# One instruction instead of four for the high part of a split weight chunk, in a one-layer hybrid trunk

## What is computed

```python
def hybrid_layer(h, p, t5_table):
    xn = rms_norm(h, p["g_pre_mix"])
    z = xn @ p["w_in"] + p["b_in"]
    ...
    y_a = gla_branch(gla_q, gla_k, gla_v, gla_r, gla_a, p) @ p["w_br_gla"]
    y_b = dsa_branch(dsa_cq, dsa_ckv, idx_k, idx_w, p, t5_table) @ p["w_br_dsa"]
    y_c = mlstm_branch(ml_q, ml_k, ml_v, ml_o, ml_i, ml_f, p) @ p["w_br_ml"]
    mix = jax.nn.sigmoid(gate_a) * y_a + jax.nn.sigmoid(gate_b) * y_b + jax.nn.sigmoid(gate_c) * y_c
    h = h + rms_norm(mix @ p["w_out"], p["g_post_mix"])
    xn = rms_norm(h, p["g_pre_mlp"])
    u = jnp.square(jax.nn.relu(xn @ p["w_up"]))
    return h + rms_norm(u @ p["w_down"], p["g_post_mlp"])
```

## Time and profile before

| what | value |
|---|---|
| median of 3 runs | 1406.42 us (1404.33 to 1410.87) |
| the profiled execution, its own time | 1403.23 us |
| its span, from first to last instruction | 1401.5 us |
| mean granted TensorE clock | 0.984 |
| TensorE matmuls busy | 1354.8 us, 97% |
| VectorE busy | 592.5 us, 42% |
| GpSimd busy | 894.7 us, 64% |

### The profile page before, as it was taken

One profiled execution on the slowest core, in us unless ns is written; L12 is line 12 of the kernel. 1 busy time (PEld: TensorE's weight loads), 2 busy tenths in 40 slices (PEclk: granted clock), 3 DMA queues, 4 the chain that ended last, 5 costly groups with the idle time before them and its releaser, 6 DMA issues.

```text
span 1401.5 us, 18053 instructions
## 1 busy us (share of the span) xinstructions
PE 1354.8 (97%) x6611; PEld 1065.3 (76%) x6611; DVE 592.5 (42%) x1135; ACT 387.9 (28%) x796; POOL 894.7 (64%) x1452
## 2 busy tenths in 40 slices
PE   6999899999999999999999999999989999999997
PEld 4866666657887877778887787788768888888886
DVE  3147888541364756622463654223151111222224
ACT  4333365430012333233131331241241111121322
POOL 8475500005764553658884775689678888999992
PEclk9998899999999999999999999999999999999999
DMA  6862200002321211222331321243223333222221
GB/s 174 213 229 61 61 1 1 16 0 70 97 71 38 74 46 46 75 62 76 105 100 52 97 76 54 75 154 117 90 64 102 90 101 109 90 101 95 90 91 60
DMA packets 165710, 116.54 MB, mean 83 GB/s; under 512 B 11832, under 2 KB 146078, under 8 KB 165622
## 3 DMA queue, kind: packets, MB, share of 16 engines
q1 hardware_dynamic: 161142, 108.43, 26.5%
q10 hardware_dynamic: 4480, 6.95, 1.6%
HBM read 113.21 MB, written 7.52 MB: 86 GB/s over the span
## 4 chain that ended last, share of the span: by engine, by line
PE 83%; DVE 9%; DMA 3%; POOL 2%; issue 1%; ACT 1%; SPq 0%; DVEq 0%; ACTq 0%; POOLq 0%
PE GP L1588 38%; PE PA L1624 8%; PE GP L1624 6%; PE GP L1603 6%; PE GP L1585 5%; PE GP L1764 3%; PE PA L1809 3%; PE PA L1732 3%; DMA wraw<-in_w_in 3%; POOL wlo L559 1%; PE GP L1762 1%; PE GP L1749 1%; PE PA L1807 1%; DVE S L1120 1%; PE PA L1796 1%
## 5 line engine op out<-in xcount | busy, mean ns | idle before, releaser
L554 POOL TENSOR_SCALAR whi<-wraw 128x256 fp32r<-128x256 f32 x712 | 345.3, 511 | 380.2 <-PE GP L1588 208.7
L559 POOL TENSOR_TENSOR wlo<-wraw,whi 128x256 fp32r<-128x256 f32 x712 | 540.6, 791 | 14.8
L1588 PE MATMUL GP<-xh,whi 128*128 128x512 f32 x368 | 153.0, 416 | 2.9 <-DVE xl L1080 1.4
L1588 PE MATMUL GP<-xl,whi 128*128 128x512 f32 x368 | 148.1, 402 | 0.0
L1588 PE MATMUL GP<-xh,wlo 128*128 128x512 f32 x368 | 147.3, 400 | 0.0
L1588 PE MATMUL GP<-nh,whi 128*128 128x512 f32 x256 | 101.2, 395 | 0.7 <-DVE nl L1525 0.7
L1588 PE MATMUL GP<-nl,whi 128*128 128x512 f32 x256 | 101.3, 396 | 0.0
L1541 DVE TENSOR_TENSOR ul<-U,uh 128x512 fp32r<-128x512 f32 x64 | 48.3, 792 | 123.1 <-ACT uh L1010 123.1
L1588 PE MATMUL GP<-nh,wlo 128*128 128x512 f32 x256 | 99.8, 390 | 0.0
L1545 DVE TENSOR_TENSOR U<-U 128x512 f32<-128x512 f32 x32 | 26.0, 811 | 149.9 <-ACT U L1014 149.9
L1588 PEld LDWEIGHTS GP<-xh,whi 128*128 128x128 f32 x368 | 71.1, 193 | 21.4 <-issue 3.0
(11 more groups left out here) (332 smaller groups left out, 2809.9 us busy)
## 6 DMA issues: line engine op xcount, KB each, us to landing
wraw<-in_w_in SPq DMA_DIRECT2D x75, 512.0 KB, 3.8
wraw<-in_w_up SPq DMA_DIRECT2D x32, 512.0 KB, 4.0
wraw<-in_w_down SPq DMA_DIRECT2D x32, 512.0 KB, 3.5
line_rows<-bias_line SPq DMA_DIRECT2D x1, 5240.0 KB, 25.3
table<-line_rows SPq DMA_DIRECT2D x1, 4224.0 KB, 14.6
wraw<-in_w_br_dsa SPq DMA_DIRECT2D x8, 512.0 KB, 4.0
wraw<-in_w_br_gla SPq DMA_DIRECT2D x8, 512.0 KB, 4.0
wraw<-in_w_br_ml SPq DMA_DIRECT2D x8, 512.0 KB, 4.0
```

The source lines that it names most:

```text
L554: part = nc.gpsimd.tensor_scalar(hi[:, at:to], src[:, at:to], 1.0, 1.0, ALU.mult, ALU.mult)
L559: part = nc.gpsimd.tensor_tensor(lo[:, at:to], src[:, at:to], hi[:, at:to].bitcast(FP32), ALU.subtract)
L1588: ins = mm(ps[0:t.m, 0:SEQ], wt[:, s0, w], av, start=st, stop=sp_)
```

## The change

The four instructions for the high part become one over all columns of the chunk. The low part stays in four. Nothing else is changed; the waits and the semaphores are the same.

```diff
-                for at in range(0, n, PIECE):
-                    to = min(at + PIECE, n)
-                    part = nc.gpsimd.tensor_scalar(hi[:, at:to], src[:, at:to], 1.0, 1.0, ALU.mult, ALU.mult)
-                part.then_inc(hi_done, 1)
+                nc.gpsimd.tensor_scalar(hi, src, 1.0, 1.0, ALU.mult, ALU.mult).then_inc(hi_done, 1)
                 pool.wait_ge(hi_done, c["r"] + 1)
```

## The result

The changed kernel takes 1407.67 us (median of 20 runs, 1405.37 to 1413.99), the kernel before 1404.01 us in the same 20 rounds (1398.26 to 1410.87). The ratio is 1.0031, with a 95% interval of 1.0017 to 1.0044: slower by 3.7 us by the two medians, inside the bound of 0.5% (7 us), and the interval doesn't hold 1, so the loss is small but real. The forecast was 1408.0 us, +1.6 us, with a range that holds 1407.67. That 1408.0 lies 0.3 us beside it is luck: the median of three runs from which it was counted, 1406.42 us, lay 2.4 us over that of 20, and the difference was put 2.1 us too low.

What follows compares the result with a forecast made beforehand. TensorE, busy for 97% of the span, was taken to bound the kernel. Gains of 1.2 us against seven places at 0.4 us, 2.8 us, gave +1.6 us on the 1406.4 us median: 1408.0 us, range 1401.5 to 1413.0 us.

Steps and rivals of the forecast that it cites:

- The duration of the long instruction: GpSimd's high part: one instruction of 1024 columns was to take about 1,055 ns, against 1.52 us for four undisturbed pieces.
- VectorE's busy time up by a few us: Sign expected in the profile after: VectorE busy only a few us longer over the whole run.
- GpSimd's saving is hidden: Whole run: nearly all of GpSimd's 82 us saving lies under TensorE's products; its busy time falls to about 780 us.
- The gains of 1.2 us: TensorE's two waits for a low part vanish: 0.8 us near 64 us and 0.4 us near 1007 us.
- GLA: One meeting of the high part with VectorE on the path in each of four GLA heads, 0.4 us each.
- The norms: Norms before the MLP: two high parts, at 1022.52 and 1028.77 us, hold up VectorE on the chain, 0.4 us each.
- mLSTM: One place only, the first convolution, behind which TensorE waits: a loss of 0.4 us.
- Elsewhere VectorE's delay is hidden under TensorE's products, which leave 0.5 us idle in 348: Outside the seven counted places, VectorE's delays were to cost nothing, since TensorE is almost never idle from 632 to 980 us.
- if TensorE waits in a stage in which it is now busy throughout: One of the prediction's own signs of being wrong: new TensorE waits in a stage without idle time before.
- The price of a meeting: Cost of one high part meeting VectorE on the path: 0.4 us taken, from bounds of 0 to 1.8 us.
- One `cv` of 1.6 to 1.9 us in the first convolution: Sign expected in mLSTM's first convolution: `cv` with one duration near 1.6 to 1.9 us in place of 0.80 us.
- The rival of VectorE held up at every GLA chunk: Half of GLA's 30 high parts hold up VectorE, 13.5 us; with norms and convolution +15 us, 1421 us; chance 0.13.

## Why the prediction was right, and where its steps were not

- *The duration of the long instruction* was right: 1,046 ns measured, 1,055 ns worked out.
- *VectorE's busy time up by a few us* was wrong by much: 45 us. Nearly all of it is hidden, which is why the forecast could stand.
- *GpSimd's saving is hidden* was right. Its busy time fell by 105 us, from 894.7 to 789.3 us, and no stage became shorter by it. The forecast of about 780 us was good.
- *The gains of 1.2 us* were a third there for sure. The wait near 1007 us (0.4 us) is gone in all three profiles of the changed kernel. The one near 64 us, 0.8 us in the first profile, was 1.8 us in two more of the kernel before and 0, 1.5 and 2.3 us in the changed one; it hangs on when a load lands, and one profile can't tell it.
- *GLA*: four places at 0.4 us were 1.6 us in the sum; the waits for `KL` grew by 1.6 us, those for `QQ` by 0.3 us, and the stage at full clock by 2 us. The size was right and the places were not: 8 waits for `KL` have become 12, and the one of 2.4 us has become shorter ones. *The norms*: 0.8 us in the sum, and 0.5 us measured, of which 0.2 us stay in the length of the stage.
- *mLSTM* is the term that was mis-sized. The sum had one place there, the first convolution, at 0.4 us. There were three, near 705, 785 and 835 us in the kernel before (703, 785 and 837 us in the changed one), with 5.5 us of waits in all. The step that failed reads "Elsewhere VectorE's delay is hidden under TensorE's products, which leave 0.5 us idle in 348": it took a busy TensorE for cover. A TensorE that never waits says only that nothing was late, not by how much it was early. The room was 0.43, 0.35 and 0.14 us at the three places. By its own list of signs the prediction was wrong here: "if TensorE waits in a stage in which it is now busy throughout" is what happened.
- *The price of a meeting* was put near the low end, 0.4 us. Where it counted it was about 1.8 us, the upper end: from 3.97 to 5.75 us for five instructions. Both parts of that bound were real, the hold (0.45 us there, 0.66 us in the run with eight low pieces) and the instructions that come to stand beside low pieces, four of them and not two, at 0.33 us each. One `cv` of 1.6 to 1.9 us in the first convolution didn't come: there the high instruction met the scans before it, and three `cv` took 1.12 to 1.13 us beside low pieces.
- The rival of VectorE held up at every GLA chunk had the right mechanism in the wrong stage. In GLA the whole price was 2 us, and not 13.5 us.

The sum of the waits, 1.6 + 0.3 + 0.5 + 5.5 less 0.4 us, is 7.5 us (the wait for `vh`, 0.5 us, is gone, and one of 0.3 us for `um` has come), and the half-clock stretch behind the first wait for `zc` adds 1.5 us (below). The three profiles of each kernel lie 8.7 us apart in their mean span (1408.0 against 1399.3 us), but the medians of 20 runs only 3.7 us. The single runs of the kernel before spread over 12.6 us and of the changed one over 8.6 us. A part of the gap is the granted clock. Its mean over a run was 0.984, 0.989 and 0.987 in the three profiles of the kernel before, where the median of its 58 later runs is 0.983: two of the three profiles show some of its quickest runs. The 20 runs of the changed kernel have a median clock of 0.986. Among all runs with 0.985 to 0.987, the medians are 1402.2 us (16 runs of before) and 1407.5 us (17 of after), so at a like clock the change costs about 5.3 us. The clocks of the 20 runs of before that stand beside the changed kernel are not on record, so whether its higher clock is chance or comes from the change is open. The right total of the forecast, +1.6 us for +3.7 us, is so partly luck: a gain that held by a third, a small price at seven places in the sum and a large one at three in fact, and a clock that may have taken some of the loss away.

## What to carry to other kernels

Where GpSimd and VectorE work beside each other and take turns, what a meeting costs is GpSimd's turn less the gap that VectorE leaves anyway (0.25 us here). Cutting GpSimd's work finely where VectorE's chain is near the path, and coarsely where it isn't, was worth 0.7% here against the kernel before; which part of this the coarse cut elsewhere has wasn't told apart from the clock. And before a delay is called hidden under a busy engine, measure the room: the time between the end of what the engine needs and the engine's start, at each hand-over, not its idle time. When two kernels are compared by single profiles, compare their granted clocks first.

## What was not expected of the hardware

- *Matmuls of the same form run at different pitches, fixed for a whole stage.* In the up projection 24 matmuls of 128x512 took 5.49 us (228.9 ns from start to start, the mean over 24) in all profiles but the first of the changed kernel, where they took 5.60 us (233.3 ns), at full granted clock and, but for the first 50, for all of the stage's 768 matmuls. That made 181.8 us of 178 us. In the down projection all profiles show 233.3 ns. What sets it is open; the change doesn't, since the same kernel showed both.
- *The stretch at half clock after the top-k stage varies.* There TensorE's granted clock falls to 1.2 GHz at two waits for VectorE (1.9 and 1.7 us, near 160 and 163 us in the first profile of before), and stays there for 6.8 to 20.5 us in different profiles (17.1 us in the first profile of before, 6.8 us in the first of after), though from 167 to 180 us TensorE is busy for all of 13.00 us. The attention stage is 141.6 us long with a short one and 147.5 us with the longest.
- *A wait can cost more than itself.* Behind the first wait for `zc`, 1.9 us, the granted clock was at half for 3.4 us in every profile of the changed kernel: 16 matmuls of 128x256 started 0.213 us apart and not 0.118 to 0.12 us, which made the stage 1.5 us longer. Behind the waits of 1.2 and 1.3 us at the same place, in the kernels with a quarter of the high part and with two high instructions, it stayed full.
- *GpSimd and VectorE take turns.* Four high pieces beside a busy VectorE took 3.35 us in place of 1.52 us, while VectorE lost next to nothing, since a turn of such a piece (0.27 us) fits between two of VectorE's instructions. The Trainium skill, SBUF — State Buffer, section "Who interferes with whom", describes an exclusive hold of the shared ports for a whole instruction. The ends agree with it: beside the long high instruction `on` ends 0.54 us after it, at 768.10 us behind 767.56 us in the changed kernel and at 771.42 us behind 770.88 us in the one with eight low pieces. The durations in the profile overlap all the same (an `on` alone takes 0.75 us), so it is the turns and not the durations that add up.
